# Turning the context's rows inside a down projection, and making its modulated tiles inside another

## What is computed

```python
# block 1, each layer, first and last sublayer
h = modulate(x, g_norm[l, 0], mod[:, 0], mod[:, 1])
x = x + 0.5 * mod[:, 2][:, None, :] * swiglu(h, w_ffn1_gu[l], w_ffn1_down[l])
...
# block 2, first layer: the context enters here for the first time
a_ctx = modulate_2(h_ctx, csh1, csc1)        # t * (1.0 + scale) + shift
y, yc = mla_mixer(a_lat, a_ctx, ...)
```

## Time and profile before

| what | value |
|---|---|
| three runs, us | 3924.23, 3916.10, 3915.02 |
| span of the profiled execution, us | 3921.6 |
| TensorE (PE) matmuls | 3758.5 us busy, 96%, 26315 instructions |
| VectorE (DVE) | 2033.1 us, 52% |
| ScalarE (ACT) | 1428.4 us, 36% |
| GpSimd (POOL) | 1695.7 us, 43% |
| mean granted TensorE clock | 0.978 of full speed |

### The profile page before, as it was taken

How to read it: one execution, slowest core, us unless ns; L and a number is a source line. 1 busy time by engine, 2 the same in 40 slices (tenths; PEclk the granted TensorE clock), 3 DMA queues, 4 the chain that set the end, 5 groups by cost and what they waited for, 6 DMA issues and landing times.

```text
span 3921.6 us, 67361 instructions
## 1 busy us (share of the span) xinstructions
PE 3758.5 (96%) x26315; PEld 3132.3 (80%) x26315; DVE 2033.1 (52%) x3403; ACT 1428.4 (36%) x2032; POOL 1695.7 (43%) x1343
## 2 busy tenths in 40 slices
PE   6999999999999999999999998999999999999998
PEld 5878878888888877888776666887879888888887
DVE  5443677344545567655454455668657333433232
ACT  3322353322432244422234442343434533435232
POOL 2444434454455434445540012355557743424442
PEclk9999999999999999999999999999999999999998
DMA  5453524444445444344320003244344522212221
GB/s 187 149 159 127 161 89 131 145 154 136 154 129 161 133 126 119 130 132 151 94 68 14 14 24 98 78 133 144 121 136 151 161 72 77 72 44 94 89 94 55
DMA packets 560085, 441.72 MB, mean 113 GB/s; under 512 B 60396, under 2 KB 558077, under 8 KB 559613
## 3 DMA queue, kind: packets, MB, share of 16 engines
q1 hardware_dynamic: 559869, 438.67, 36.2%
HBM read 431.58 MB, written 2.83 MB: 111 GB/s over the span
## 4 chain that ended last, share of the span: by engine, by line
PE 76%; issue 8%; DVE 8%; POOL 3%; ACT 3%; DMA 1%; SPq 1%; DVEq 0%; ACTq 0%; POOLq 0%
PE ps_all L2383 22%; PE ps_all L2385 21%; PE ps_all L2384 21%; DVE acc L3097 2%; POOL w_lo L923 2%; DMA g_raw<-in_w_mod_dram 1%; PE ps_all L2368 1%; PE ps_all L2077 1%; PE ps_all L2097 1%; PE ps_all L2363 1%; PE ps_all L2364 1%; PE ps_all L1954 1%; PE ps_all L2339 1%; DVE acc L3099 1%; PE ps_all L2133 1%
## 5 line engine op out<-in xcount | busy, mean ns | idle before, releaser
L923 POOL TENSOR_TENSOR w_lo<-raw,w_hi 128x512 fp32r<-128x512 f32 (+2 forms) x1124 | 1403.5, 1280 | 2001.1 <-ACT w_hi L1494 1926.7
L2383 PE MATMUL ps_all<-h_hi,w_hi 128*128 128x512 f32 (+1 forms) x2680 | 1052.1, 393 | 19.8 <-POOL w_lo L923 12.7
L2385 PE MATMUL ps_all<-h_hi,w_lo 128*128 128x512 f32 (+1 forms) x2680 | 1038.8, 388 | 0.0
L2384 PE MATMUL ps_all<-h_lo,w_hi 128*128 128x512 f32 (+1 forms) x2680 | 1038.6, 388 | 0.0
L1494 ACT ACTIVATE w_hi<-raw 128x2048 fp32r<-128x2048 f32 (+4 forms) x278 | 472.8, 1701 | 1389.1 <-PE ps_all L2385 1309.5
L2383 PEld LDWEIGHTS ps_all<-h_hi,w_hi 128*128 128x128 f32 x2680 | 509.3, 190 | 126.8 <-issue 22.0
L3097 DVE SCALAR_TENSOR_TENSOR acc<-g_raw,c_col,acc 128x256 f32<-128x256 f32 x1104 | 607.7, 617 | 1.7
L2385 PEld LDWEIGHTS ps_all<-h_hi,w_lo 128*128 128x128 f32 x2680 | 508.2, 190 | 104.2
L2384 PEld LDWEIGHTS ps_all<-h_lo,w_hi 128*128 128x128 f32 x2680 | 509.4, 190 | 99.1
L2383 PE MATMUL ps_all<-hid_hi,w_hi 128*128 128x512 f32 (+1 forms) x1282 | 481.0, 375 | 20.9 <-DVE hid_lo L3212 13.7
L2385 PE MATMUL ps_all<-hid_hi,w_lo 128*128 128x512 f32 (+1 forms) x1282 | 473.8, 370 | 0.0
(11 more groups left out here) (424 smaller groups left out, 5151.8 us busy)
## 6 DMA issues: line engine op xcount, KB each, us to landing
raw<-in_w_ffn_gu_dram SPq DMA_DIRECT2D x88, 1024.0 KB, 5.1
g_raw<-in_w_mod_dram SPq DMA_DIRECT2D x72, 1024.0 KB, 5.4
raw<-in_ffn_w_in_dram SPq DMA_DIRECT2D x66, 1024.0 KB, 5.0
g_raw<-in_ada_w_dram SPq DMA_DIRECT2D x48, 1024.0 KB, 5.2
raw<-in_w_ffn_down_dram SPq DMA_DIRECT2D x32, 768.0 KB, 4.8
raw<-in_w_ffn_down_dram SPq DMA_DIRECT2D x32, 640.0 KB, 4.3
raw<-in_ffn_w_out_dram SPq DMA_DIRECT2D x24, 768.0 KB, 4.8
raw<-in_ffn_w_out_dram SPq DMA_DIRECT2D x24, 640.0 KB, 4.4
```

The lines of the kernel that those rows point to most:

```text
L923: ins = nc.gpsimd.tensor_tensor(v(w_lo), v(raw), v(w_hi).bitcast(F32), ALU.subtract)
L2383: nc.tensor.matmul(o, whi, mhi, start=first, stop=False)
L2384: nc.tensor.matmul(o, whi, mlo, start=False, stop=False)
L2385: return nc.tensor.matmul(o, wlo, mhi, start=False, stop=last)
```

## The change

The step "context" is taken out of the list. The first `dn` step gets a flag `turns_rows`: after its iteration 0 (both panels and the reduction) TensorE makes all 16 transposes without waiting between them, into four PSUM banks (0 to 3, two tiles in each), and ScalarE copies four times 128 x 512 to `hc`, behind the `split_hi` of panel (1, 1). The second `gu` step waits for the copies before its first panel instead of its second.

The step "mod_h" is taken out too. The last `dn` step of block 1 gets `ctx_in`: tile 0 is made after panel (0, 0), tiles 1 and 2 after (0, 1), and tiles 3 to 7 after (1, 0) to (3, 0), one each. On VectorE each stands behind the addition of that panel's result, on ScalarE behind the `split_hi` issued there, and on GpSimd behind the `split_lo` issued there, which is that of the panel two further on. The buffer is a new `ctx_t` instead of `full_t`. The loops on ScalarE and GpSimd are unrolled there. At the end of the step VectorE waits until all eight subtractions are done.

```diff
+def ctx_in_of(i, j):
+
+    n = 2 * i + j
+    return (0,) if n == 0 else (1, 2) if n == 1 else (n + 1,) if n < KD - 1 else ()
@@ plan_block1
-                  dn_step(w_dn[0], 0, m(2), free[1])]
-        if l == 0:
-            steps += [dict(kind="context", totals=dict(hc_tr=KD, hc_in=KD))]
-        steps += [
+                  dn_step(w_dn[0], 0, m(2), free[1], turns_rows=l == 0),
                   gu_step(w_gu[0], 1, False, free[2]),
...
-            steps += [mods_of(0), norm_step("mod_h", CTX_COL + KD, CTX_COL, N=C, ctx=True, dst="c0")]
-        steps += [dn_step(w_dn[1], 1, m(8), free[3], sums="square")]
+            steps += [mods_of(0)]
+        steps += [dn_step(w_dn[1], 1, m(8), free[3], sums="square", ctx_in=(CTX_COL + KD, CTX_COL) if l == DEPTH - 1 else None)]
@@ GpSimd, one(i, last) of the step
                         split_lo(ahead(st, i, j, last))
+                        for k in ctx_in_of(i, j) if ctx_in else ():
+                            h_low(b, k, k, C, ctx_t[:, k % 2, :], (c0_hi, c0_lo))
@@ ScalarE, one(i, last) of dn, behind split_hi
+                        for k in ctx_in_of(i, j) if ctx_in else ():
+                            act.wait_ge(sem["h_full"], b["h_full"] + k + 1)
+                            nc.scalar.activation(c0_hi[:, k * C:(k + 1) * C], ctx_t[:, k % 2, :], ACT.Copy).then_inc(sem["h_hi"], 1)
+                        if turns_rows and j and isinstance(i, int) and i == 0:
+                            for k in range(KD // 2):
+                                act.wait_ge(sem["hc_tr"], b["hc_tr"] + k + 1)
+                                nc.scalar.activation(hc[:, 2 * k * C:(2 * k + 2) * C], ps_all[:, k, :], ACT.Copy).then_inc(sem["hc_in"], 1)
@@ TensorE, new, called after iteration 0 of the first dn step
+        def turn_rows(b):
+
+            pe.wait_ge(sem["c_rows_in"], 16)
+            pe.wait_ge(sem["product"], b["product"])
+            for k in range(KD):
+                for t in range(2):
+                    at = (k % 2) * C + t * P
+                    ins = nc.tensor.transpose(ps_all[:, k // 2, at:at + P], c_rows[:, t, k * P:(k + 1) * P], ident[:, :])
+                if k % 2:
+                    ins.then_inc(sem["hc_tr"], 1)
@@ TensorE, gu
-                        if st is streams[2] and j == 1:
+                        if st is streams[2]:
-                            pe.wait_ge(sem["hc_in"], KD)
+                            pe.wait_ge(sem["hc_in"], KD // 2)
@@ VectorE, one(i, last) of dn, behind the addition
+                        for k in ctx_in_of(i, j) if ctx_in else ():
+                            if k >= 2:
+                                dve.wait_ge(sem["h_ready"], b["h_ready"] + k - 1)
+                            scale, shift = (modc[:, c0 + k:c0 + k + 1] for c0 in ctx_in)
+                            nc.vector.tensor_scalar(ctx_t[:, k % 2, :], hc[:, k * C:(k + 1) * C], scale, shift, ALU.mult, ALU.add).then_inc(sem["h_full"], 1)
@@ VectorE, end of the dn step
+                if ctx_in:
+                    dve.wait_ge(sem["h_ready"], b["h_ready"] + KD)
```

More of the change, by code:

```diff
@@ L162, in squares_before_tail, with dn_step @@
     return dict(squared=KD - n, pre_summed=1)
-def dn_step(w, half, gate, gemv, N=S, ctx=False, sums=None):
+def ctx_in_of(i, j):
+    n = 2 * i + j
+    return (0,) if n == 0 else (1, 2) if n == 1 else (n + 1,) if n < KD - 1 else ()
+def dn_step(w, half, gate, gemv, N=S, ctx=False, sums=None, turns_rows=False, ctx_in=None):
     k0, nk = HALVES[half]
     wp = weight_panels(w)
-    return dict(kind="dn", iters=KD // 2, shapes=[(nk, P)] * 2, nk=nk, gate=gate, gemv=gemv, N=N, ctx=ctx, sums=sums,
+    return dict(kind="dn", iters=KD // 2, shapes=[(nk, P)] * 2, nk=nk, gate=gate, gemv=gemv, N=N, ctx=ctx, sums=sums, turns_rows=turns_rows, ctx_in=ctx_in,
                 dma=lambda i, j: [(None, wp[:, k0:k0 + nk, ds(j * P + i * (2 * P), P)])],
-                totals=dict(down0=KD // 2, down1=KD // 2, **(squares_before_tail(1) if sums == "square" else SUMS[sums])))
+                totals=dict(down0=KD // 2, down1=KD // 2, **(squares_before_tail(1) if sums == "square" else SUMS[sums]),
+                            **(dict(hc_tr=KD // 2, hc_in=KD // 2) if turns_rows else {}), **(dict(h_full=KD, h_hi=KD, h_ready=KD) if ctx_in else {})))
 def proj_step(dma, gate, gemvs=(), ctx_gate=None, sums=None, order=tuple(range(KD))):
@@ L537, in build @@
     r_sb = sb("r_sb", [P, S], at=spare + 8192)
+    ctx_t = sb("ctx_t", [P, 2, C], at=spare + 8192)
     row_in = sb("row_in", [P, row_tiles, P], at=hid)
@@ L994, in _ @@
                 context = st["kind"] == "dn" and inner and inner["ctx"]
+                ctx_in = st.get("ctx_in")
                 def one(i, last):
@@ L998, in one @@
                         split_lo(ahead(st, i, j, last))
+                        for k in ctx_in_of(i, j) if ctx_in else ():
+                            h_low(b, k, k, C, ctx_t[:, k % 2, :], (c0_hi, c0_lo))
                         for k in range(4 * i + 2 * j - 6, 4 * i + 2 * j - 4) if context and (1, 1) <= (i, j) <= (3, 0) else ():
                             h_low(inner["base"], k, k, C, full_t[:, k % 2, 0:C], dst_of(inner))
-                Chain(pool, sem["pool_chain"]).loop(st["iters"], 0, one, unroll=st["iters"] if context else 0)
+                Chain(pool, sem["pool_chain"]).loop(st["iters"], 0, one, unroll=st["iters"] if context or ctx_in else 0)
     def rms_act(st, b, act, split_hi_part):
@@ L1543, in _ @@
                 split_hi((streams[0], 0, 1))
[L1544 to L1547, removed]
             elif st["kind"] == "norm":
@@ L1638, in _ @@
                 inner, update = st.get("inner"), st.get("update")
+                ctx_in, turns_rows = st.get("ctx_in"), st.get("turns_rows")
                 def one(i, last):
@@ L1669, in _ @@
                         norm_squares(inner, k)
-                ch.loop(st["iters"], 0, one, unroll=st["iters"] if inner else 0)
+                ch.loop(st["iters"], 0, one, unroll=st["iters"] if inner or ctx_in else 1 if turns_rows else 0)
             elif st["kind"] == "mixer":
@@ L2419, in _ @@
                                 ins.then_inc(sem["square_summed"], 1)
-            elif kind == "context":
-                pe.wait_ge(sem["c_rows_in"], 16)
-                pe.wait_ge(sem["product"], b["product"])
-                for k in range(KD):
-                    if k >= 2:
-                        pe.wait_ge(sem["hc_in"], k - 1)
-                    for t in range(2):
-                        ins = nc.tensor.transpose(ps_u[:, k % 2, t * P:(t + 1) * P], c_rows[:, t, k * P:(k + 1) * P], ident[:, :])
-                    ins.then_inc(sem["hc_tr"], 1)
             elif kind == "rms":
@@ L2523, in one @@
                         sum_squares(inner)
+                    if st["turns_rows"] and isinstance(i, int) and i == 0:
+                        turn_rows(b)
                 if inner and inner["ctx"]:
@@ L2526, in _ @@
                 if st["sums"] != "mean":
-                    Chain(pe, None).loop(st["iters"], 0, one, unroll=st["iters"] if inner and inner["ctx"] else 0)
+                    Chain(pe, None).loop(st["iters"], 0, one, unroll=st["iters"] if inner and inner["ctx"] else 1 if st["turns_rows"] else 0)
                 else:
```

2 lines of the change are left out of this document (1 added, 1 removed).

## The result

The changed kernel takes 3929.4 us (median of 9 runs, 3924.2 to 3933.6); the kernel before, on the same chip, 3920.8 us (9 runs, 3915.0 to 3928.6). The ratio is 1.0024, with a 95% interval of 1.0015 to 1.0033: 8.6 us or a quarter of a per cent slower. That is inside the band of 0.3% that I called "no change", but the forecast of 3916.3 us and its range up to 3922 missed it. The profiled execution has a span of 3923.9 us, to the earlier trace rows come from one of 3921.6 us.

The account below looks back on a forecast made before the run. Matmuls fill 96% of the span, so only TensorE's standstill or half clock could be won. Transposes +1.4 and tiles -1.2 (-7.0 + 5.8) gave +0.2 on 3916.1: 3916.3 us, own range 3913.7 to 3921.1, wider range 3908 to 3922.

Parts of the forecast that it names:

- A, the transposes as a delay passed on: First down step to first gate/up panel: transposes' 2.0 us passed on through bias list and load, 2.0 half clock; net +1.4.
- B, front: Panel (1, 0) of block 1's last down step: the 4.07 us wait and half clock after it go, -7.0 us.
- B, end: End of block 1's last down step: tile 7's late subtraction costs 4.4 us, half clock 1.4 more, +5.8 us.
- The lower bound of 4.2 us: End of block 1's last down step: least cost of tile 7's late subtraction if the clock stays up, 4.2 us.
- Both stalls are won: Rival, first gate/up panel and block 1's last down step: both stalls vanish, -7.6 us, 3908.5 us; chance 0.13.
- The clock falls in the down panel: Rival: half clock in panel (1, 0) of the first down projection, behind 16 transposes; sum +2.2, 3918.3 us; chance 0.20.
- The front stall stays: Rival, block 1's last down step: panel (1, 0)'s split still 4 us late, sum +7.2, 3923.3 us; chance 0.05.
- the sum: Whole kernel: +1.4 for the transposes and -1.2 for the tiles make +0.2 us, added to the median: 3916.3 us.

Follow-up runs that it names:

- e7: Kernel before with only the modulated tiles moved, tiles 6 and 7 both behind panel (2, 1): 3916.2 us, ratio 0.9989 to the kernel before.
- e13: Changed kernel with transposes behind iteration 3, tiles 6 and 7 behind panel (2, 1), plus 32 idle transposes behind iteration 0: 3915.2 us, ratio 0.9989.
- e0: The kernel before, unchanged, timed again against itself: 3920.5 us, ratio 1.0001.
- e1: The changed kernel timed again against the kernel before: 3927.8 us, ratio 1.0021.
- e15: Kernel before with only the context rows moved, 8 transposes behind iteration 0 and 8 behind iteration 3: 3922.5 us, ratio 1.0010.
- e2: Kernel before with only the context rows' transposes moved, as in the change; tiles left in their own step: 3926.7 us, ratio 1.0018.
- e3: Kernel before with only the modulated tiles moved, as in the change; context step kept: 3921.0 us, ratio 1.0004.
- e6: Kernel before with only the context rows moved, the 16 transposes behind iteration 3 of the first down step: 3919.4 us, ratio 0.9998.
- e9: Kernel before with only the context rows moved, each of the 16 transposes behind iteration 0 made twice: 3922.6 us, ratio 1.0009.
- e14: Kernel before with only the context rows moved, 24 transposes behind iteration 0, half the tiles made twice: 3927.6 us, ratio 1.0020.
- e5: Kernel before with 16 unused transposes behind iteration 0 of layer 1's first down step, at 1180 us: 3925.1 us, ratio 1.0012.
- e12: Changed kernel with transposes behind iteration 3, tiles 6 and 7 behind panel (2, 1), plus 16 idle transposes behind iteration 0: 3914.8 us, ratio 0.9995.
- e4: Kernel before with 16 unused transposes behind iteration 0 of the first down step, context step kept: 3924.9 us, ratio 1.0008.
- e10: Changed kernel with transposes behind iteration 3, tiles 6 and 7 behind panel (2, 1), bias list inside the second gated step: 3911.2 us, ratio 0.9979.

## Why the prediction was wrong

**A, the transposes as a delay passed on: right in its order.** 16 transposes lengthen the step by 1.61 us (2.0 forecast; 1.8 was the lower end). The list and the load follow by 1.6 us and the split by 1.33, with a wait for `w_lo` of 5.1 us (5.7 forecast). The panel then starts 0.04 us later than before, not 0.8: besides the 0.4 us of the transposes, the low part was read 0.2 us too late (its four pieces ended at 277.66 before, not at half of the eight, 277.90). Half clock costs the panel 1.9 us (2.0 forecast). The net price, +1.4 forecast, is +0.5 in the first pair of executions and +1.6 over ten.

**B, front: right.** -7.0 forecast; from mark 164 to 168, which ends at panel (2, 1)'s copy, 35.08 us became 28.15, -6.9.

**B, end: right.** +5.8 forecast, 6.9 - 1.4 = +5.5 measured: a wait of 4.31 us on VectorE (4.4), then 3.85 on TensorE (4.4), which does four of the eight matmuls of the sum before it has to wait. From the other four to the spread it takes 3.14 us (1975.96 to 1979.10), and before 1.84 (1980.39 to 1982.23): 1.3 us of half clock (1.4 forecast). e7 took it away. The lower bound of 4.2 us has no working in the prediction; its own terms, with the clock up, give 4.4.

**The rivals.** "Both stalls are won" did not happen, though e7 shows how half of it could. "The clock falls in the down panel" did not happen: the granted clock over all of it is 1.00.

```profile
222.00:260.00 38.00, 38.00 (x183) 31.89 (x182) 17.58 (x27) 9.39 (x9) 17.45 (x17) 1.00 0.49 145
```

Even the 32 transposes of e13, 3.69 us in a row, leave it so, in the 6 us from 222.00 (they start at 221.84):

```profile
222.00:228.00 6.00, 6.00 (x44) 5.54 (x44) 6.00 (x8) 1.17 (x1) 4.58 (x4) 1.00 0.23 68
```

The Trainium skill (TensorE: Matmul & The Clock Gate, Part 4: PE-mode transpose) has it that transposes don't count as work for the gate. Amid matmuls no run here shows a price of that. "The front stall stays" did not happen.

**The step that failed is the sum:** "the two places are the same in each run, so I add it to the median". The two places are nearly the same; the rest of the kernel is not. In the mean of its runs a kernel here spends 147 to 174 us at half clock, in stretches behind some dozens of waits of 1 to 7 us, and how much of each such stretch is at half clock changes when the work ahead of it is shifted by 1 or 2 us. With the clock, the waits behind change as well. The sum put all of this at nothing; it gave +0.2 us for both parts where the runs say +8.6 and +8.1, and in e0 and e1 all of the loss lies behind mark 172.

How much of it is the clock? In the table, over the changed kernel and e0 to e15 without the two with the list moved, mean time and mean half-clock time go together (correlation 0.96 over fifteen, 0.94 with the two), at 0.6 us for each us of it, where 0.5 is what half clock alone costs. From 157 us (before) to 172 (the changed kernel) this would make 15 x 0.5 = 7.5 us of the 8.6. The two traces of e0 and e1 do not bear that share out: 164 and 168 us at half clock, which is worth 1.8 us, and the rest in longer waits. How the loss divides between the two is open.

The Trainium skill (TensorE: Matmul & The Clock Gate, Part 1: The HAM clock gate) says that how long a kernel runs at the lower clock after its start varies from run to run, and puts the cost of this ramp below 1% of a typical kernel's span. The runs agree that the time at half clock varies (granted clocks of 0.978 to 0.981 over the eleven of e0). Here half clock comes back behind many waits, and its 157 us cost up to 78 us, 2% of the span.

What is shown: the loss comes with part A at iteration 0 (e2, e3, e6); it is not in the work (e6), nor in proportion to the delay (e9, e14); and it lies in stretches that nobody edited (e0 and e1 trace by trace). That a bare delay costs more than its length is clear in one of four trials (e5, 3.4 us more, se 1.4), not clear in e12 (2.2, 1.5) and e4 (1.7, 1.6), and not so in e13. That re-timing is the whole of A's loss is thus argued, and not shown. What stays open: why 16 and 24 transposes hit a bad pattern and 32 do not, so whether any new edit would hit one cannot be told ahead; and whether e2's excess over e4, 3.9 us with a standard error of 2.1, is more than the different stall that e4 keeps.

**The base was off too.** Median 3916.1 of three runs against 3920.8 measured beside the changed kernel: 4.7 of the 13.1 us of my error, and the four later occasions (3918.9 to 3920.3) side with the latter. The profiled execution, 8 us above that median, could have warned me.

## What to carry to other kernels

Where a kernel has many short stalls, add to any sum over the edited places a spread for the stalls that are merely shifted. Here the mean times less what the places themselves show come out between -2 us (e9) and +8 (the changed kernel), mostly above zero. Read each run's granted clock and TensorE's waits beside its time, and take a trace from an execution at its kernel's median. Put moved work into a wait that is there anyway, and on a queue ahead of what comes late there: two positions turned 1.0021 into 0.9983. And ask of a long list of transfers which load stands behind it.

## What the runs showed of the hardware

- 16 fp32 transposes of 128x128 amid matmuls cost 1.65 us, 32 cost 3.42 (mark 14 to 16 in e12 and e13: 18.48 and 20.25 against 16.83): 0.10 to 0.11 us each. The granted clock stays at 1.00 over the 32.
- One stretch of 728 matmuls lasts 87.65, 89.02 or 90.89 us at a granted clock of 1.00, 0.98 or 0.96, with the other engines' work the same.
- A stall that is taken away can leave the time as it was: e10 won 5.0 us in its place and 0.8 +- 1.4 in all.
- At nearly the same half-clock time two executions can be 7.8 us apart: e0 and e1, with TensorE standing still 6.8 us longer behind mark 172.
